# A three-block network on one core: bias broadcast, first recurrence factors, gla's log decay, mLSTM heads and a head norm moved

## The chip, the cores and the metric

One core of a Trainium2 chip runs the whole program as one launch. The time is the device time of that core in microseconds (us). The kernel before took 3819.36, 3821.92 and 3830.99 us in three runs, median 3821.92.

## The reference

Batch 1, 512 tokens, 1024 features, float32. Three blocks follow one another. The first puts 16 meta tokens ahead (528 in all) and merges an RWKV-7 recurrence with differential attention, then an MLP. The second has a gated convolution and a sparse attention with position biases. The third mixes an mLSTM, a gated linear attention (gla) and a gated delta net, then an MLP. What matters here, cut down:

```python
# block 1, RWKV-7: per head a 64x64 state over 528 tokens
S = S * w_t + (S a_t) b_t^T + v_t k_t^T;   y_t = S r_t
# block 2: position bias of a head at a distance
bias = rel_bias[t5_bucket(distance)]
# block 3, mLSTM (4 heads of 128): weights from scalar gates, divided by their sum
h = sigmoid(mo) * mlstm(q / sqrt(128), k, v, li, log_sigmoid(lf));  h = head_rmsnorm(h)
# block 3, gla: log decay per feature and token, summed along the tokens
lg = log_sigmoid(llr @ w_gla_lr + b_gla) / 16;   b = cumsum(lg)
S = exp(b_L) * S + sum_s (k_s * exp(b_L - b_s)) v_s^T
```

## The kernel before

Activations lie with features on the 128 partitions and tokens along them. A matmul of full precision is made of three of rounded float32 (h_hi by whi, h_lo by whi, h_hi by wlo): ACT rounds a slab of weights of 8 x 128 x 128 (whi), VectorE or POOL makes the rest (wlo). The program is a row of stages; each ends with a barrier of all engines, and inside one the engines wait on semaphores. Each engine takes its instructions in the order in which they are written; DMAs are issued from SP's queue, some from ACT's.

**opening** (L1898) loads x on SP, norms it and writes the pair h. Three small tables on ACT's queue give, by TensorE, the biases by distance (`row`, 8 heads x 640) and by residue (`cmp_row`). SP waits for `row` and writes it to DRAM 128 times over (`far`, 2.6 MB, from 8 partitions, L1928), then `near` (L1930). ACT squares x, copies the rows, makes the root, issues eleven loads of constants (L1964), and then makes the eight h_hi copies (L1967). VectorE's products (L1991) and low parts (L1988) alternate with these.

**rwkv_project** (L569) makes 27 projection tiles of 528 tokens: three for the low-rank inputs, then three (r, k, v) for each of eight groups of two heads. SP's queue carries for each group i: three weights for group i+2 (L612; one of them into the buffer `first`), a wait for the group's factors, the stores of factors, bonus and gate (L630 to L632), and the vectors of group i+2 (L615, L616). ACT rounds the weights (L723) between the evictions of tiles (L731) and the group's sigmoids, gate copy (L757), exponentials (L759 to L762) and root (L764). VectorE makes the factors and the bonus (L785 to L821); POOL the wlo.

**rwkv_tiles** (L825) runs the recurrence in chunks of 64 tokens. SP loads the factors of a group into one of three buffers f (L890, L891), after VectorE has padded them (L1181); TensorE transposes them first (L907).

**chain** (L97) is the helper for all later projections: slabs of weights in a ring of buffers, TensorE in slab order (L233), whi (L249) and wlo (L331) two or three slabs ahead, eviction of a tile with its scale by VectorE (L381). A `side` object puts further steps behind each slab s on TensorE, ACT and VectorE. HeadNorm (L1467) is one: it norms mLSTM's four heads in the last chain: square by ACT at s = 0, 3, 6, 9 (L1492), sum by TensorE at the same s (L1483), mean (L1503) and root (L1495) at s + 1, reciprocal and product (L1506, L1510) at s + 2. GateRows (L2296) is another, in the chain ahead of gla: it makes the scalar gates of four heads.

**gla** (L2480) starts with the log decay: TensorE's four products of 16 rows (L2541), bias (L2692), Abs, Exp and Ln by ACT (L2625 to L2629), scaling and four scans (L2697 to L2700), the far factors (L2703, L2634, L2706), then seven levels of decays. Of a level the argument is made by VectorE or POOL (L2527), two exponentials by ACT (L2640, L2641), two products by VectorE (L2711, L2712). ACT copies values (vt, L2632) and keys (kt, L2657), VectorE sums up the states (L2734 to L2736).

**mlstm** (L2362) runs four heads in a loop. POOL copies the head's keys, values, selector and scaled queries (L2423 to L2426); TensorE spreads the gate rows (L2395, L2396), transposes the values, makes four scores (L2404) and four pairs of values (ps_o L2412, ps_d L2413); ACT makes em, vt, four exponentials and one sigmoid; VectorE the arguments (L2456), weights (L2463) and the division (L2467 to L2471). POOL and TensorE begin the next head when `done` is reached:

```python
                with pe.Fori(0, 4) as h:
                    pe.wait_ge(fixed, h + 1)
                    pe.wait_ge(done, h)
```

## Time and profile before

| | |
|---|---|
| runs | 3819.36, 3821.92, 3830.99 us |
| profiled execution | 3828.68 us, span 3826.9 us |
| TensorE matmul busy | 3395.8 us (89%) |
| TensorE weight load busy | 2776.4 us (73%) |
| VectorE busy | 2032.3 us (53%) |
| ACT busy | 1235.7 us (32%) |
| POOL busy | 214.0 us (6%) |
| mean granted TensorE clock | 0.922 |

The profile is of one execution. Busy time is the sum of an engine's instructions; the busiest engine needn't be what a given stage waits for, so each stage is read for itself. A granted clock of 1.00 is 2.4 GHz, 0.50 is 1.2 GHz. The stages of interest lie at 0 to 75.9 us (opening), 75.9 to 309 (projections), 309 to 615 (recurrence), 2566 to 2681 (the chain ahead of gla), 2682 to 2787 (gla), 2970 to 3052 (mlstm) and from 3180 on (the last chain).

### The profile page before, as it was taken

To read this page: it belongs to the slowest core of one execution; us is meant where nothing else is said; L and a number is where in the kernel's file an instruction comes from. 1 tells how busy PE (TensorE), PEld (TensorE's weight loads), DVE (VectorE), ACT (ScalarE), POOL (GpSimd) and SP (SyncE) were. 2 spreads that over 40 slices of the span, in tenths; PEclk is the share of its full clock that TensorE was granted. 3 is DMA by queue.
4 is the path that set the end of the run, shared out by engine and by line. 5 is a ranking of instruction groups with operands and counts; after the bars stand their busy time and mean duration, and the time that the engine had idled before them with its cause. 6 is when DMAs were issued, how large, how long until landed. Compare 5 with 4: busy or idle time off the path is not lost. (4 is left out here: it accounts for less than half of the span.)

```text
span 3826.9 us, 57163 instructions
## 1 busy us (share of the span) xinstructions
PE 3395.8 (89%) x24046; PEld 2776.4 (73%) x24046; DVE 2032.3 (53%) x3290; ACT 1235.7 (32%) x2144; POOL 214.0 (6%) x187
## 2 busy tenths in 40 slices
PE   2996899988999999989999998969499698999998
PEld 1986888955888887757777777857378386878886
DVE  2885564555355344676546775354646445465342
ACT  2552233345333233223333222232422324333231
POOL 1321220010000000000000000000100120000000
PEclk9997898988999999975799999989699689999999
DMA  5332112201222322610122223322022002232221
GB/s 114 119 140 68 46 32 91 88 1 39 94 93 94 99 94 69 172 35 12 45 78 88 88 88 94 93 65 72 2 88 91 0 2 83 77 106 95 97 99 56
DMA packets 99340, 287.81 MB, mean 75 GB/s; under 512 B 19618, under 2 KB 23842, under 8 KB 97040
## 3 DMA queue, kind: packets, MB, share of 16 engines
q1 hardware_dynamic: 92456, 268.71, 21.9%
q10 hardware_dynamic: 6632, 15.47, 1.6%
q8 instruction: 191, 3.13, 0.3%
q14 instruction: 61, 0.50, 0.0%
HBM read 264.22 MB, written 19.89 MB: 74 GB/s over the span
## 5 line engine op out<-in xcount | busy, mean ns | idle before, releaser
L233 PE MATMUL acc<-h_hi,whi 128*128 128x512 f32 x1992 | 800.9, 402 | 74.4 <-DVE wlo L425 50.2
L233 PE MATMUL acc<-h_hi,wlo 128*128 128x512 f32 x1992 | 791.6, 397 | 0.0
L233 PE MATMUL acc<-h_lo,whi 128*128 128x512 f32 x1928 | 769.9, 399 | 0.0
L233 PEld LDWEIGHTS acc<-h_hi,whi 128*128 128x128 f32 x1992 | 379.1, 190 | 184.2 <-DVE wlo L425 52.6
L331 DVE TENSOR_TENSOR wlo<-wbuf,whi 128x1024 fp32r<-128x1024 f32 (+3 forms) x277 | 318.6, 1150 | 268.6 <-ACT whi L249 266.0
L233 PEld LDWEIGHTS acc<-h_hi,wlo 128*128 128x128 f32 x1992 | 379.4, 190 | 87.8
L233 PEld LDWEIGHTS acc<-h_lo,whi 128*128 128x128 f32 x1928 | 367.0, 190 | 86.9 <-issue 3.1
L249 ACT ACTIVATE whi<-wbuf 128x1024 fp32r<-128x1024 f32 (+3 forms) x277 | 274.5, 991 | 358.5 <-PE acc L233 335.3
L233 PE MATMUL acc<-arena_round,whi 128*128 128x512 f32 x736 | 236.9, 393 | 4.8 <-DVE arena_round L391 4.8
L331 DVE TENSOR_TENSOR wlo<-ahead,whi 128x1024 fp32r<-128x1024 f32 (+3 forms) x132 | 152.3, 1154 | 137.0 <-ACT whi L249 136.3
L249 ACT ACTIVATE whi<-ahead 128x1024 fp32r<-128x1024 f32 (+3 forms) x132 | 131.4, 996 | 178.6 <-PE acc L233 173.1
L658 PE MATMUL acc<-h_hi,whi 128*128 128x264 f32 x432 | 127.9, 296 | 65.2 <-POOL wlo L646 65.2
L233 PEld LDWEIGHTS acc<-arena_round,whi 128*128 128x128 f32 x736 | 139.4, 190 | 34.9 <-DVE arena_round L391 5.7
L233 PE MATMUL acc<-arena_round,wlo 128*128 128x512 f32 x416 | 162.9, 392 | 0.0
L233 PE MATMUL acc<-gates_round,whi 128*128 128x512 f32 x384 | 141.2, 395 | 3.0 <-DVE gates_round L391 1.8
L397 DVE TENSOR_TENSOR x<-acc,x 128x512 f32<-128x512 f32 x64 | 44.3, 692 | 178.4 <-PE acc L233 178.4
L658 PEld LDWEIGHTS acc<-h_hi,whi 128*128 128x128 f32 x432 | 83.0, 192 | 69.1 <-POOL wlo L646 65.9
L233 PE MATMUL acc<-gates_round,wlo 128*128 128x512 f32 x320 | 125.5, 392 | 0.0
L658 PE MATMUL acc<-h_lo,whi 128*128 128x264 f32 x432 | 123.9, 287 | 0.0
L658 PE MATMUL acc<-h_hi,wlo 128*128 128x264 f32 x432 | 123.9, 287 | 0.0
L1415 PE MATMUL acc<-h_hi,whi 128*128 128x264 f32 x384 | 115.9, 302 | 1.2 <-DVE wlo L1453 1.2
L282 ACT ACTIVATE val<-tmp 128x512 f32<-128x512 f32 x64 | 40.5, 632 | 216.7 <-DVE tmp L393 216.7
(730 smaller groups left out, 6365.6 us busy)
## 6 DMA issues: line engine op xcount, KB each, us to landing
wbuf<-in_mlp_out SPq DMA_DIRECT2D x46, 512.0 KB, 3.3
wbuf<-in_mlp_in SPq DMA_DIRECT2D x45, 512.0 KB, 3.3
wbuf<-in_w_gates SPq DMA_DIRECT2D x38, 512.0 KB, 3.4
wbuf<-in_ffn_up SPq DMA_DIRECT2D x29, 512.0 KB, 3.4
wbuf<-in_w_qkv SPq DMA_DIRECT2D x23, 512.0 KB, 3.6
rwkv_factors<-factors SPq DMA_DIRECT2D x8, 1320.0 KB, 4.6
f<-rwkv_factors SPq DMA_DIRECT2D x8, 1280.0 KB, 6.7
ahead<-in_mlp_in SPq DMA_DIRECT2D x19, 512.0 KB
```

The source lines that it names most:

```text
L233: mm = nc.tensor.matmul(acc[t % NB][:, 0:T], wt[s % ring][:, k - a, :], xt, start=(kx == 0 and q == 0), stop=(kx == job.K - 1 and q == 2))
L249: copy(whi[s % ring][:, 0:size(s), :], wbuf[s % ring][:, 0:size(s), :], ACT.Copy).then_inc(hi_ready, 1)
L282: copy(val[t % 2][:], tmp[t % 2][:], ACT.Square)
L331: TT(wlo[s % ring][:, 0:size(s), :], wbuf[s % ring][:, 0:size(s), :], whi[s % ring][:, 0:size(s), :].bitcast(F32), ALU.subtract).then_inc( ...
L397: TT(job.dst[n], ps, job.other[n], ALU.add).then_inc(evicted_d, 1)
L658: mm = nc.tensor.matmul(acc[n % 2][:, hf, 0:H], wt[n % R][:, kx, :], xt[:, kx, at], start=(kx == 0 and q == 0), stop=(kx == 7 and q == 2))
L1415: mm = nc.tensor.matmul(acc[n % NB][:, h, 0:H], wt[n % R][:, k, :], xt[:, k, h * H:(h + 1) * H], start=(k == 0 and q == 0), stop=(k == 7 a ...
```

## The change

- `far` isn't written in the opening. `row` stays resident, and rwkv_project writes it in eight pieces of 16 copies, each behind the stores of a group on SP's queue.
- The eleven constants are loaded by SP, behind `first`, instead of by ACT.
- The first group's factors are loaded at the end of rwkv_project into `early`, which lies in the place of y's tiles 2 to 7; POOL pads it. rwkv_tiles loads groups 1 to 7 only, and its memset of y goes.
- HeadNorm's sum moves to s + 1, mean and root to s + 2, reciprocal and product to s + 3.
- gla's log decay is made by a new side object, GlaGates, in the chain ahead of gla, in the places of z and o that are still free; GateRows' scratch moves into z too.
- mlstm's loop is written out with the heads overlapped; POOL's copies go, the scaling is in the weights, and the sigmoid is one instruction.

```diff
 # rwkv_project, SP
                     sp.dma_start(gate_scr[:, i, :], gates[i % 2][:]).then_inc(stored[i % 2], 16)
+                    sp.dma_start(far[:, 16 * i:16 * i + 16, :], row[:].rearrange("h (a w) -> h a w", a=1).broadcast_to([8, 16, 640])).then_inc(far_out, 16)
                     if i + 2 < 8:
                         vectors(i + 2)
+                sp.dma_start(early[:, :, 0:RM], fac_scr[0, :, :, 0:RM]).then_inc(early_in, 16)
+                sp.dma_start(early[:, :, RM + 48:], fac_scr[0, :, :, RM:T1]).then_inc(early_in, 16)
+                sp.wait_ge(early_in, 32)
                 for b in range(2):
                     sp.wait_ge(stored[b], 4 * 48)
+                sp.wait_ge(far_out, 16 * 8)
 # rwkv_tiles
+        def f_of(i):
+            return early if i == 0 else fs[i % 3]
-                for i in range(8):
-                    f = fs[i % 3]
-                    if i >= 3:
+                for i in range(1, 8):
+                    f = f_of(i)
+                    if i > 3:
                         sp.wait_ge(y_out, 2 * (i - 2))
-                nc.vector.memset(y[:, :, 0:RM], 0.0)
 # HeadNorm
-        if s < 12 and s % 3 == 0:
+        if s < 12 and s % 3 == 1:
             pe.wait_ge(self.sq_ready, s // 3 + 1)
...
-        elif s < 12 and s % 3 == 2:
+        elif 0 < s < 13 and s % 3 == 0:
+            h -= 1
             dve.wait_ge(self.root_ready, h + 1)
 # opening
-                sp.wait_ge(row_out, 1)
-                sp.dma_start(far, row[:].rearrange("h (a w) -> h a w", a=1).broadcast_to([8, P, W])).then_inc(stored, 16)
+                for name in names:
+                    sp.dma_start(c[name][:], a[name]).then_inc(const_in, 16)
...
-                for name in names:
-                    act.dma_start(c[name][:], a[name]).then_inc(const_in, 16)
 # GlaGates, a new side (ACT's DMAs of its weights at s = 2 left out)
+    def pe(self, pe, s, stat):
+        if s in (6, 8):
...
+            for q in range(2):
+                h = s - 6 + q
+                mm = self.nc.tensor.matmul(stat[q][:], self.wl[:, h * P:(h + 1) * P], self.lr, start=True, stop=True)
+    def act(self, act, s):
+        elif s == 9:
+            act.wait_ge(self.lin_ready, 4)
+            copy(pos, self.lin, ACT.Abs).then_inc(self.abs_ready, 1)
+            act.wait_ge(self.abs_ready, 1)
+            copy(pos, pos, ACT.Exp, scale=-1.0).then_inc(self.pow_ready, 1)
+        elif s == 10:
+            copy(pos, pos, ACT.Ln, bias=1.0).then_inc(self.ln_ready, 1)
+        elif s == 14:
+            copy(self.far[:], self.far[:], ACT.Exp).then_inc(self.far_exp, 1)
+            copy(self.dec[:], self.cum[:].rearrange("p h (n t) -> p h n t", t=GW)[:, :, :, GW - 1], ACT.Exp)
+    def dve(self, dve, s):        # s: what
+        # 7, 9: bias, two heads each   8: queries scaled   11: STT and the factor 1/16
+        # 12, 13: two scans each       14: far's argument  16: far times the keys
 # mlstm, TensorE
+                prelude(0)
+                scores(0, 0)
+                scores(0, 1)
+                for h in range(4):
+                    values(h, 0)
+                    scores(h, 2)
+                    values(h, 1)
+                    scores(h, 3)
+                    if h < 3:
+                        prelude(h + 1)
+                    values(h, 2)
+                    if h < 3:
+                        scores(h + 1, 0)
+                    values(h, 3)
+                    if h < 3:
+                        scores(h + 1, 1)
 # mlstm, ACT: sigmoid of all four heads first, then per head em, vt and four exponentials
+                copy(z[:, 12:16, :], z[:, 12:16, :], ACT.Sigmoid).then_inc(sig_ready, 1)
 # mlstm, VectorE
+                rows_of(0)
+                args(0, 0)
+                args(0, 1)
+                for h in range(4):
+                    weights(h, 0)
+                    args(h, 2)
+                    weights(h, 1)
+                    args(h, 3)
+                    weights(h, 2)
+                    if h < 3:
+                        rows_of(h + 1)
+                        args(h + 1, 0)
+                    weights(h, 3)
+                    if h < 3:
+                        args(h + 1, 1)
+                    divide(h)
```

`prelude` is the two spreads of gate rows and the transposes of the values; em, vt and mb have two buffers now, ps_o and ps_d one, and `values(h, 0)` waits for `done` of the head before. In gla all that the new side makes is gone, with its waits: TensorE begins with the transposes of the values, ACT with their copies, VectorE with the argument of level 0.

## Rows read from the trace of the kernel before

**Rows 1.** Timeline of the opening: start, duration (us), engine, line, operation, [idle before]

```profile
11.50 0.85 SPq L1928 DMA_DIRECT2D bias_by_distance<-row  x1
...
12.97 19.01 SPq L1930 DMA_DIRECT2D bias_by_residue<-cmp_row  x1
...
19.26 1.45 DVE L1991 SCALAR_TENSOR_TENSOR squares<-x,norm_w,rstd 128x528 f32<-128x528 f32 x2
...
64.98 1.18 ACT L1967 ACTIVATE h_hi<-squares 128x528 fp32r<-128x528 f32 x2 [49.24 <-issue]
...
75.93 0.36 SPq L612 DMA_DIRECT2D wbuf<-in_w_rwkv  x1
```

**Rows 2.** DMA queues from 20 to 60 us: queue, packets, MB, share

```profile
q1 hardware_dynamic: 768, 1.97, 46.6%
```

**Rows 3.** Projections, one group's timeline, and ACT's idle time before L723

```profile
187.33 0.33 SPq L630 DMA_DIRECT2D rwkv_factors<-factors  x1
...
197.71 1.06 ACT L723 ACTIVATE whi<-first 128x1024 fp32r<-128x1024 f32 x1 [2.46 <-DMA first<-in_w_rwkv]
...
211.06 0.71 DVE L821 TENSOR_TENSOR bonus<-za,factors 128x528 f32<-128x528 f32 x1
...
  DMA first<-in_w_rwkv: 6.9, 5
```

**Rows 4.** Timeline from the projections to the recurrence

```profile
301.78 0.32 SPq L630 DMA_DIRECT2D rwkv_factors<-factors  x1
...
308.95 0.77 DVE L1181 MEMSET f<- 128x240 f32 x3 [7.20 <-PEq L42]
...
309.75 0.62 SPq L890 DMA_DIRECT2D f<-rwkv_factors  x1
...
317.28 1.97 PE L907 MATMUL psA<-ident,f 128*128 128x128 f32 x8 [22.07 <-DMA f<-rwkv_factors]
```

**Rows 5.** Busy time by stretch: length, PE, PEld, DVE, ACT, POOL, PEclk, DMA share, GB/s

```profile
2640.00:2660.00 20.00, 20.00 (x88) 16.17 (x87) 7.56 (x8) 4.25 (x4) 0.00 (x0) 1.00 0.26 87
2681.00:2720.00 39.00, 11.58 (x25) 5.75 (x26) 22.54 (x15) 14.50 (x13) 7.59 (x2) 0.53 0.01 1
```

**Rows 6.** Timeline: end of the chain ahead of gla, and gla's start

```profile
2680.08 0.69 DVE L381 TENSOR_TENSOR z<-acc,scale 128x512 f32<-128x512 f32 x1 [4.88 <-PE acc L233]
...
2681.69 1.80 POOL L2678 MEMSET scores<- 128x2048 f32 x1 [1801.46 <-POOLq L42]
...
2684.22 5.48 PE L2541 MATMUL psL<-small,wl 16*128 16x512 f32 x6 [4.18 <-DMA w<-in_norm_gla]
...
2701.18 1.07 ACT L2632 ACTIVATE vt<-psT 128x512 f32<-128x512 f32 x2
...
2711.71 5.77 DVE L2527 TENSOR_TENSOR ring<-cum 128x2048 f32<-128x2048 f32 x1
...
2719.60 1.21 DVE L2711 TENSOR_TENSOR ring<-ring,z 128x1024 f32<-128x1024 f32 x1
...
2728.12 2.29 DVE L2527 TENSOR_TENSOR ring<-cum 128x2048 f32<-128x2048 f32 x1
```

**Rows 7.** mlstm: timeline of a head, and the clock of one stretch

```profile
2972.67 1.47 PE L2395 MATMUL ps_b<-rows,sel 4*128 4x512 f32 x2 [2.48 <-POOL qs L2426]
...
2985.16 0.69 DVE L2467 TENSOR_TENSOR den<-ps_d,em 128x512 f32<-128x512 f32 x1 [1.11 <-PE ps_d L2413]
...
2991.68 2.04 PE L2395 MATMUL ps_b<-rows,sel 4*128 4x512 f32 x2 [6.65 <-DVE o_m_plain L2471]
...
3005.20 0.69 DVE L2467 TENSOR_TENSOR den<-ps_d,em 128x512 f32<-128x512 f32 x1 [1.11 <-PE ps_d L2413]
...
3000.00:3002.00 2.00, 2.00 (x6) 1.03 (x5) 0.35 (x2) 1.47 (x3) 0.00 (x0) 0.84 0.00 0
```

**Rows 8.** Last chain: waits (total, times, longest), and a stretch

```profile
PE stat L1483 <- ACT sums L1492: 10.1, 4, 3.0
...
3192.00:3195.00 3.00, 3.00 (x7) 1.87 (x6) 1.23 (x1) 0.35 (x1) 0.00 (x0) 0.50 0.37 122
```

More of the change, by code:

```diff
@@ L566, with rwkv_project @@
 LEVELS1 = math.ceil(math.log2(RC))
-def rwkv_project(nc, c, w, first, h, fac_scr, chunk_decay, bonus_scr, gate_scr):
+def rwkv_project(nc, c, w, first, row, far, h, fac_scr, early, chunk_decay, bonus_scr, gate_scr):
     NT, R = 27, 3
@@ L1895, in dve, with opening @@
                 TT(self.a[:, i, :], self.a[:, i, :], self.rstd[:], ALU.mult).then_inc(self.norm_ready, 1)
-def opening(nc, a, c, both, x, h, far, near, first):
+def opening(nc, a, c, both, x, h, row, near, first):
     H = T1 // 2
-    W = far.shape[2]
+    W = row.shape[1]
     M = near.shape[1] * near.shape[2]
@@ L1957, in _ @@
                 act.wait_ge(rows_ready, 1)
-                copy(row[:].rearrange("h (a w) -> h a w", a=2), ps_r[0:8, :, 0:W // 2], ACT.Copy).then_inc(row_out, 1)
+                copy(row[:].rearrange("h (a w) -> h a w", a=2), ps_r[0:8, :, 0:W // 2], ACT.Copy)
                 act.wait_ge(rows_ready, 2)
@@ L2330, in act @@
             act.wait_ge(self.end_ready, 1)
-            copy(rows[:, 7, :], self.end[:], ACT.Exp)
+            copy(rows[:, 7, :], self.end, ACT.Exp).then_inc(self.exp_done, 1)
     def dve(self, dve, s):
@@ L2386, in _, with prelude, scores, values @@
             def _(pe):
+                def prelude(h):
+                    if h > 0:
+                        pe.wait_ge(mb_ready, h)
+                    nc.tensor.matmul(ps_b[:], c["head_sel"][:, h, :], rows[:, 1, :], start=True, stop=True).then_inc(b_ready, 1)
+                    if h > 0:
+                        pe.wait_ge(em_ready, h)
+                    nc.tensor.matmul(ps_e[:], c["head_sel"][:, h, :], rows[:, 2, :], start=True, stop=True).then_inc(e_ready, 1)
+                    if h > 0:
+                        pe.wait_ge(v_copied, h)
+                    for j in range(TN):
+                        mm = nc.tensor.transpose(ps_v[:, j * P:(j + 1) * P], z[:, 8 + h, j * P:(j + 1) * P], c["ident"][:])
+                    mm.then_inc(v_ready, 1)
+                def scores(h, j):
+                    g = TN * h + j
+                    if g > 1:
+                        pe.wait_ge(pt_ready, g - 1)
+                    nc.tensor.matmul(ps_k[g % 2][:, 0:T2 - j * P], z[:, 4 + h, j * P:(j + 1) * P], z[:, h, j * P:T2], start=True,
+                                     stop=True).then_inc(kq_ready, 1)
+                def values(h, j):
+                    g, n = TN * h + j, T2 - j * P
+                    if j == 0:
+                        pe.wait_ge(v_copied, h + 1)
+                        if h > 0:
+                            pe.wait_ge(done, h)
+                    pe.wait_ge(pt_ready, g + 1)
+                    nc.tensor.matmul(ps_o[:, j * P:T2], vt[h % 2][:, j * P:(j + 1) * P], pt[g % 2][:, 0:n], start=(j == 0), stop=(j == TN - 1))
+                    nc.tensor.matmul(ps_d[:, j * P:T2], c["ones"][:], pt[g % 2][:, 0:n], start=(j == 0), stop=(j == TN - 1)).then_inc(o_ready, 1)
                 for j in range(TN):
@@ new lines, in _, with prelude @@
+                copy(z[:, 12:16, :], z[:, 12:16, :], ACT.Sigmoid).then_inc(sig_ready, 1)
+                def prelude(h):
+                    act.wait_ge(e_ready, h + 1)
+                    if h > 1:
+                        act.wait_ge(done, h - 1)
+                    copy(em[h % 2][:], ps_e[:], ACT.Exp).then_inc(em_ready, 1)
+                    act.wait_ge(v_ready, h + 1)
+                    if h > 1:
+                        act.wait_ge(o_ready, TN * (h - 1))
+                    copy(vt[h % 2][:], ps_v[:], ACT.Copy).then_inc(v_copied, 1)
@@ L2471, in _ @@
                     TT(o[:, h, :], ps_o[:], den[:], ALU.mult).then_inc(done, 1)
-                    chain.close()
+                    dve.wait_ge(done, h + 1)
+                rows_of(0)
+                args(0, 0)
+                args(0, 1)
+                for h in range(4):
+                    weights(h, 0)
[7 more added lines that the diff above has]
+                    weights(h, 3)
+                    if h < 3:
+                        args(h + 1, 1)
+                    divide(h)
@@ L3242, in first_block @@
             decay = resident(nc, m2, "chunk_decay", [P, 8, RN + 1])
+            early = y[:, 2:8, :].rearrange("p k t -> p (k t)")[:, 0:5 * (RM + 48 + RN * RC)].rearrange("p (f t) -> p f t", f=5)
             with ExitStack() as m3:
                 first = resident(nc, m3, "first", [P, 8, P])
-                opening(nc, a, c, both, x, h, far, near, first)
-                rwkv_project(nc, c, a["w_rwkv_1"], first, h, factors, decay, bonus, gate)
-            rwkv_tiles(nc, c, y, factors, decay)
+                row = resident(nc, m3, "row", [8, 640])
+                opening(nc, a, c, both, x, h, row, near, first)
+                rwkv_project(nc, c, a["w_rwkv_1"], first, row, far, h, factors, early, decay, bonus, gate)
+            rwkv_tiles(nc, c, y, factors, early, decay)
         o, o_lo = overlaid(nc, m, "o", [P, 8, T2])
```

298 lines of the change are left out of this document (145 added, 153 removed).

## The prediction

> **What bounds the kernel now.** I read the page's engine table first. TensorE is busy 3395.8 us of 3826.9 (the table above), so an edit pays only where TensorE waits, or where a stage has little for it. Then I read timeline and waits of each stage that the diff touches, asking which wait ends last.
>
> In the opening, `row` (the biases by distance) leaves by one DMA at 11.50, and the next issue on SP's queue takes 19.01 us. ACT has eleven loads of constants to issue ahead of its h_hi copies; these start at 64.98, though VectorE had the input of the first ready half way through its row at 19.26. The projections begin at 75.93 [rows 1]. No engine bounds this stage; the broadcast does: from 20 to 60 us its queue moved 768 packets [rows 2], 19.2 per us.
>
> In the projections a tile takes about 24 us, and the loop is tight: SP issues the stores of a tile (187.33), then vectors, then weights; ACT waits for the weights in `first` until 197.71, and only behind that copy come the exponentials that VectorE needs; VectorE's bonus ends at 211.77. ACT waited for this DMA five times, in all five tiles that have it [rows 3]. So its landing already sets the time of such a tile.
>
> **The change part by part.** The profiled execution took 3828.68 us (its span 3826.9), 6.8 above the median of 3821.92; I take differences from its rows and apply them to the median.
>
> *Opening.* ACT issues no constants, and no broadcast is in flight. VectorE's first product is there at 20.0, so h_hi starts at some 20.1 instead of 64.98, and what hangs on it, up to 75.93, follows at the same distance: **-44.9**. Eleven loads move to SP behind `first`: at up to 0.85 us an issue [rows 1] they are out within 10 us of x's, and their 1.6 MB lands before VectorE's last low part near 30, which covers them. Without that cover they would cost perhaps 5.
>
> *Broadcast in eight pieces.* A piece has 8 x 16 packets of the same 2,560 bytes, from the same eight partitions: 128 packets at 19.2 per us are 6.67 us. It stands on SP's queue behind a tile's stores and ahead of its vectors and weights. Bounds of the delay to `first`: 0, if it trickles beside them, and 19.0, if an issue behind it blocks as in [rows 1]. I take 6.67, since what is queued must drain either way, and 128 packets do that in it. ACT is in order: behind its wait for `first` stand the gate copy, both exponentials and the root for kn; VectorE waits for those, SP's next stores for VectorE. In the tile of [rows 3] `first` comes 10.4 after the stores, and from there to the bonus's end it is 14.1; a later landing moves those 14.1 whole. Five tiles (behind the last three pieces no weights follow): 5 x 6.67 = **+33.4**. TensorE idles longer in them; a fallen clock would add up to 2 a tile, which goes into the range.
>
> By the Trainium skill (DMA: Bandwidth & Descriptors, Queues, rings and completion order) each DMA engine takes the descriptors of one issuer's ring in order, which speaks against this place for the pieces; by it the delay is the whole piece, and if the trace of after shows the weights landing as early as now, the sum lacks the 33.4. The Trainium skill (SBUF — State Buffer, Door 1) gives about 27 GB/s for each port that a DMA's partitions reach, and two ports for partitions 0 to 7: an estimate of 6.0 us a piece and 30 in all, where the row says 33.4.
>
> *Early factors.* Before, the last stores are issued at 301.78, the next stage's VectorE starts at 308.95, its first load is issued at 309.75 and its first transpose runs at 317.28, after that DMA [rows 4]: 15.5 us. Now a piece (6.7) and the early load stand behind the stores (about 6.0 to land, as the stage then ends). Of the 7.5 from that load's issue to the transpose I take 5, since it queues behind others, and 1.8 for the change of stage: 19.5, **+4**. Bounds: -3, if the piece runs beside the stores, and +7. The memset of y that goes and the padding that POOL gains lie under other waits and cost nothing, less than 0.3 uncovered. The later factors had no wait in the trace and get none.
>
> *Log decay.* Slabs of this chain are 5.57 us apart (0.69 of eviction and 4.88 idle before it [rows 6]), TensorE full; VectorE is busy 7.56 and ACT 4.25 of 20 us. What moves is most of gla's first 39 us: 22.54 of VectorE less the 5.77 of a level's argument that stays, 16.8, and some 10 of ACT's 14.50 [rows 5, 6]. Over nine slabs (50 us) that fits between low parts, which are made two slabs ahead: 0, and about 2 without that slack. TensorE's four products do come onto its path: three took 5.48 at half clock [rows 6], so four take 7.3 there and **+3.7** at full. In gla the first products of level 0 came at 2719.60, 37.9 after a start at 2681.7 [rows 6]. Now VectorE begins with the level's argument (2.29 where POOL isn't beside it, as at 2728.12). ACT makes four vt copies behind the transposes (some 4.5 us from the start: two took 1.07, and they alternate with as long transposes) and two exponentials (2.1, from the argument's end at 2717.48 to the products): products at +6.6, that is 31.3 earlier. The states after them no longer wait for kt's source; they end 1.2 earlier still. Net 3.7 - 32.5 = **-28.8**, between -24 and -31.
>
> *mLSTM heads.* A head takes 20.04 us (2985.16 to 3005.20): 6.5 of division with TensorE idle, then 13.5 of TensorE with hardly a gap, at half clock (1.2 GHz) until inside 3000 to 3002 and full (2.4 GHz) after [rows 7]. The next head's values still wait for `done`, as ps_o and ps_d are single. So on the path stay the division, all values, scores 2 and 3, and the next head's prelude and score 0, which are only issued earlier, ahead of the last values. Score 1 goes under the division (384 columns where 512 took 2.04 at half clock, so about 0.8 at full); the first weights (an operation of 512 like the 0.69 of [rows 7], and a hop), which lay beside TensorE's work, step onto the path. Nothing per head. At the start POOL's copies go (TensorE waited 2.48), but ACT now makes the whole sigmoid with two table loads ahead of em: of the 2.5 about 1.4 is left, **-1**. Bounds: -16, if the clock stays full, and +5, if ACT's new order holds up the first head.
>
> *Head norm.* TensorE waits for ACT's squares four times, 10.1 us in all, and runs at 0.50 for 3 us after the first [rows 8], which costs 1.5. A slab later the squares are ready; root and reciprocal keep their distance. **-11.5**.
>
> Sum: -44.9 + 33.4 + 4 - 28.8 - 1 - 11.5 = -48.8, so **3773** from the median.
>
> **Rivals.**
> *The pieces hide.* They run beside the weights. For: the old broadcast let ACT's loads through while it ran. Against: same queue, ahead of the weights, and ACT's waits of [rows 3]. Price: the 33.4 fall out, and some 4 at the hand-over: 3736.
> *mLSTM at full clock.* For: the next prelude lengthens each burst of TensorE. Against: the pause stays 6.5. Half of the some 9 us at half clock, four times, with a bit lost to VectorE: 16 in all, 3757.
> *Slower than before.* Each piece blocks SP's queue like the issue of 19.01 us, with vectors and weights behind it, in the five tiles. With a delay d they cost 5d, against 82.2 gained elsewhere: it decides from d = 16.4, and is slower by over 0.3% from 18.7. At 20 us: +17.8, 3840. Against: an eighth of the packets drains in a third of that.
> *The opening stays long*, because another load holds ACT. Nothing else is issued there on ACT's queue between x and h_hi; I give it nothing.
>
> **How the numbers follow.** Forecast 0.73, pieces hidden 0.14, full clock 0.10, slower 0.03. The likeliest gives 3773. Its bounds: a delay of 5 to 9 a tile (-8, +12), half clock in the projections (+10), gla and mLSTM (-10, +8). The range reaches down to the first rival and up to 3797. About 0.3% (11.5 us) is what a measurement of this kernel can tell from no change. The first three cases are faster, with 0.02 of them left for an unforeseen gap that ends within 0.3%: 0.95, 0.02, 0.03.
>
> **What would show it.** The projections start near 31. Their tiles 1 to 5 take 30 us instead of 24, with ACT waiting some 8 us for `first` in each, and the last two stay. The first transpose of the recurrence comes 19 to 20 after the last stores. gla's first products come 6 to 7 after its start, and its chain has four products more and no new gap. A head of mLSTM stays near 20, at half clock after each division. The last chain has no wait on squares. I am wrong if the tiles stay at 24, if a gap opens in the gla chain near slabs 9 to 12, or if the heads fall to 16.

## The result, and the profile of the changed kernel

The changed kernel takes 3765.22 us (median of four runs, 3757.46 to 3779.03), the kernel before 3822.6 on the same chip: a ratio of 0.9849, 95% interval 0.982 to 0.9879, so 57.4 us less. The forecast was 48.8 less (3773). The profiled execution took 3757.46 us (span 3755.7), the fastest of its four, where the profiled one of before took 3828.68: the two traces differ by 71.2, more than the medians.

To see where it went, I took in both traces the time at which each stage starts and subtracted. Stage lengths are in us; "forecast" is the term of the sum.

| stretch | before | after | difference | forecast |
|---|---|---|---|---|
| start to the projections | 75.9 | 31.4 | -44.5 | -44.9 |
| projections: five groups with weights behind the piece | 119.6 | 156.6 | +37.0 | +33.4 |
| projections: last two groups | 41.6 | 43.3 | +1.7 | 0 |
| last stores to first transpose | 15.5 | 17.9 | +2.4 | +4 |
| product ahead of gla, and gla | 221.4 | 189.1 | -32.2 | -28.8 |
| product ahead of mLSTM, and mLSTM | 265.6 | 256.4 | -9.1 | -1 |
| last product (head norm) | 624.0 | 611.0 | -13.1 | -11.5 |
| all other stages together | | | -13.4 | 0 |

The touched stretches sum to -57.8, close to the 57.4 of the medians. The last row I don't count to the change. Its largest entries are a stage at 1689 us (183.1 before, 177.6 after), the recurrence behind its first transpose (297.3, 293.8) and the stage behind mLSTM (127.2, 124.2). In the kernels tried below, which leave the code of these stretches as it is in the changed kernel, they took 177.6 to 186.0, 294.0 to 297.3 and 121.6 to 128.7.

The touched stretches scatter too, so each difference is that of one pair of traces. The five groups took 151.2 to 156.6 in the eight traces that have the pieces in this place and size. mLSTM itself is 83.2 before and 73.1 after. Of eight other kernels with the same mLSTM four took 73.0 and four 76.0; in these four the clock granted to TensorE falls 3.6 us after the stage's first product and is at half for 10.2 us, where in the others it falls 0.6 to 0.7 after it and is at half for 6.8.

**Opening** (answers to [rows 1]). Timeline of the changed kernel: start, duration, engine, line, operation, [idle before].

```profile
20.47 1.32 ACT L1978 ACTIVATE h_hi<-squares 128x528 fp32r<-128x528 f32 x2 [4.33 <-DVE squares L2001]
...
31.39 0.83 SPq L614 DMA_DIRECT2D wbuf<-in_w_rwkv  x2
```

ACT's first high part comes at 20.47 instead of 64.98, and waits only for VectorE. In the kernel before, beside the broadcast, ACT's loads of constants (twelve by the trace, where I had counted eleven) were slow to issue, 3.9 to 4.8 us each from the second on:

```profile
15.50 4.72 ACTq L1964 DMA_DIRECT2D ident<-in_ident  x1
...
61.07 3.86 ACTq L1964 DMA_DIRECT2D rope_swap<-in_rope_swap  x1
```

**Projections** (to [rows 3]). Timeline of SP's queue and of ACT in one group, then ACT's waits from 90 to 320 us (total, times, longest).

```profile
126.52 0.33 SPq L632 DMA_DIRECT2D rwkv_factors<-factors  x1
...
128.32 1.31 SPq L635 DMA_DIRECT2D bias_by_distance<-row  x1
129.68 1.26 SPq L617 DMA_DIRECT2D vec<-in_rwkv_vec  x1
130.98 3.38 SPq L618 DMA_DIRECT2D lora_w<-in_lora_up  x1
134.41 3.04 SPq L614 DMA_DIRECT2D first<-in_w_rwkv  x1
...
143.56 1.06 ACT L731 ACTIVATE whi<-first 128x1024 fp32r<-128x1024 f32 x1 [7.61 <-DMA first<-in_w_rwkv]
...
ACT whi L731 <- DMA first<-in_w_rwkv: 29.1, 5, 7.6
```

The weights in `first` serve ACT 17.0 us after the group's stores (10.4 before), and it waited 29.1 us for them where it waited 6.9. On average of the five groups they come 15.2 us after the stores (9.6 before). SP's issues behind the piece also take longer, 3.38 and 3.04 us.

That is 5.6 us a group; the other 1.8 lie between ACT's copy of `first` and the next stores, which takes 16.2 us on average (14.3 before). ACT's operations up to `kn` and VectorE's behind them wait for TensorE nowhere in that stretch. In each of the five groups one of VectorE's operations behind `kn` takes 2.7 to 2.9 us where it takes 0.7 alone, while POOL makes a low part beside it:

```profile
151.59 4.65 POOL L654 TENSOR_TENSOR wlo<-wbuf,whi 128x1024 fp32r<-128x1024 f32 x2 [4.53 <-ACT whi L731]
...
154.06 2.76 DVE L823 TENSOR_TENSOR kn<-kn,kk 128x528 f32<-128x528 f32 x1
```

In the group of [rows 3] the same product (L815) took 0.71 us; it took 1.02 and 1.66 in two others, beside such a low part. ACT rounds the second and third weight of the group 2.2 us apart now (150.45 and 152.67), since what it has to evict ahead of them became ready while it waited; in a group before they came 6.7 apart (180.37 and 187.09). So the low part falls among VectorE's last operations ahead of the stores. In one group of the eight traces it didn't (m2_prelude_in_pause, from 141.5 us), and the stretch took 14.1 us; in all others it took 16.1 to 16.2.

**Hand-over** (to [rows 4]). Same view.

```profile
295.84 0.32 SPq L632 DMA_DIRECT2D rwkv_factors<-factors  x1
...
298.96 1.28 SPq L638 DMA_DIRECT2D y_plain<-rwkv_factors  x1
300.28 4.22 SPq L639 DMA_DIRECT2D y_plain<-rwkv_factors  x1
...
313.77 1.94 PE L919 MATMUL psA<-ident,y_plain 128*128 128x128 f32 x8 [24.52 <-PEq L42]
```

**Start of gla** (to [rows 6]). VectorE goes straight to the first level's argument, and has its products 5.1 us after the stage's first instruction, where it was 37.9.

```profile
2670.13 1.80 POOL L2803 MEMSET scores<- 128x2048 f32 x1 [1796.78 <-POOLq L42]
2670.17 2.29 DVE L2674 TENSOR_TENSOR ring<-cum 128x2048 f32<-128x2048 f32 x1 [1.03 <-PEq L42]
...
2675.19 1.90 DVE L2819 TENSOR_TENSOR ring<-ring,z 128x1024 f32<-128x1024 f32 x1 [2.73 <-ACT ring L2766]
```

**mLSTM** (to [rows 7]). Timeline of two divisions, then the stretch around the second (columns as in [rows 5]).

```profile
2946.30 0.69 DVE L2604 TENSOR_TENSOR den<-den,z_m 128x512 f32<-128x512 f32 x1
...
2948.59 2.05 PE L2516 MATMUL ps_o<-pt,vt 128*128 128x512 f32 x2 [6.51 <-DVE pt L2593]
...
2964.09 0.69 DVE L2604 TENSOR_TENSOR den<-den,z_m 128x512 f32<-128x512 f32 x1
...
2962.00:2966.00 4.00, 0.00 (x0) 0.00 (x0) 3.90 (x4) 0.00 (x0) 0.00 (x0) 0.62 0.00 0
2966.00:2970.00 4.00, 3.62 (x5) 1.64 (x6) 1.42 (x4) 0.91 (x2) 0.00 (x0) 0.52 0.02 4
2970.00:2974.00 4.00, 4.00 (x15) 2.05 (x14) 1.33 (x3) 0.08 (x1) 0.00 (x0) 1.00 0.00 0
```

TensorE still pauses 6.5 us, but the clock is full again some 4 us after it resumes (2966.4 to 2969.8), where it had been some 9. After the three divisions it ran at half clock for 4.2, 3.4 and 3.1 us; before, for 8.9, 9.4 and 9.6. The divisions lie 17.8, 17.4 and 13.9 us apart (20.0, 20.3 and 20.4 before). In the last chain TensorE's waits list no `sums` any more ([rows 8]), only those of 4.8 and 4.1 us that both kernels have.

### The profile page after: what moved, and what is told of

The parts are those of the page before. It is cut to its first block and busy times, and to the rows that moved or that the text cites. A ratio compares the mean times of both kernels' runs of the same rounds, so it can differ in the third digit from the quotient of the medians.

```text
span 3755.7 us, 56986 instructions
## 1 busy us (share of the span) xinstructions
PE 3377.5 (90%) x24046; PEld 2765.4 (74%) x24046; DVE 2021.5 (54%) x3289; ACT 1225.3 (33%) x2135; POOL 201.8 (5%) x171
## 5 line engine op out<-in xcount | busy, mean ns | idle before, releaser
L233 PEld LDWEIGHTS acc<-h_hi,whi 128*128 128x128 f32 x1992 | 378.9, 190 | 183.4 <-DVE wlo L425 52.9
L666 PE MATMUL acc<-h_lo,whi 128*128 128x264 f32 x432 | 125.4, 290 | 0.0
L1426 PE MATMUL acc<-h_lo,whi 128*128 128x264 f32 x384 | 109.6, 286 | 0.0
```

Source lines behind the costliest of these rows:

```text
L233: mm = nc.tensor.matmul(acc[t % NB][:, 0:T], wt[s % ring][:, k - a, :], xt, start=(kx == 0 and q == 0), stop=(kx == job.K - 1 and q == 2))
L666: mm = nc.tensor.matmul(acc[n % 2][:, hf, 0:H], wt[n % R][:, kx, :], xt[:, kx, at], start=(kx == 0 and q == 0), stop=(kx == 7 and q == 2))
L1426: mm = nc.tensor.matmul(acc[n % NB][:, h, 0:H], wt[n % R][:, k, :], xt[:, k, h * H:(h + 1) * H], start=(k == 0 and q == 0), stop=(k == 7 a ...
```

## The experiments

Each kernel is the changed kernel with the edit named. Two questions led: what in the pieces costs 37 us, and why mLSTM gained nine times what I gave it.

### Where a piece stands in the queue

```diff
@@ p1_pieces_behind
                 for n in group(i + 2): weight(n)
+                sp.dma_start(far[:, 16 * i:16 * i + 16, :], ...)
                 sp.wait_ge(fac_ready, i + 1)
...
-                sp.dma_start(far[:, 16 * i:16 * i + 16, :], ...)
@@ p2_weights_ahead
-                for n in group(i + 2): weight(n)
+                for n in [*(group(2) if i == 0 else ()), *group(i + 3)]: weight(n)
                 sp.wait_ge(fac_ready, i + 1)
```

> Each piece of the broadcast is issued behind the three weights of its tile, ahead of the wait for the tile's factors, instead of behind the stores; nothing else differs from the changed kernel, in which five groups take 156.6 us (31.3 each, 23.9 before) and ACT waits 7.6 us at the longest for the weights in the first buffer. Theory A (order): the cost is that the weights stand behind the piece's packets in the queue. Then ACT's wait falls back to some 2.5 us, the five groups to about 120 to 124, and the time by 33 to 37 us, to about 3730. Theory B (shared bandwidth): the piece slows whatever moves beside it, wherever it stands. Then the stores, issued some 17 us later, meet no piece, but the second and third weight do; ACT waits for those instead, and at most 15 us come back, to about 3750 or above. Slower than the changed kernel by neither.

Measured: 3721.6 us, ratio 0.9733 (0.9704 to 0.9763). ACT's waits:

```profile
ACT whi L731 <- DMA first<-in_w_rwkv: 7.7, 5, 2.2
```

The five groups take 118.4 us, the wait is back where it was (7.7 in all, 6.9 before), and the piece, in flight beside nothing urgent, costs nothing. It was the order. The medians differ by 43.6 rather than 37. By the traces the five groups are 38.2 shorter, the last two groups 1.6, and from the last stores to the first transpose it is 11.1 us instead of 17.9, because the last piece now stands ahead of those stores.

> The three weights of a tile are issued one tile earlier, as soon as their buffers are free, ahead of the wait for the factors and the stores; the pieces stay where they are, behind the stores and ahead of the vectors. Theory A (order): the piece now delays only the stores' followers that nobody waits for, so the whole 37 us come back, and with them the waits of 2.5 us for the weights that the kernel before already had, five times: about 45 to 49 us less than the changed kernel's 3765, some 3718, with tiles of 21 to 22 us. Theory B (shared bandwidth): the weights, moved out of the piece's time, are not slowed either; the same. Rival C: the vectors and the product of the next tile (they stand behind the piece) are the next to be late; they were issued two tiles ahead, so I give that little: then a wait for the vectors appears in front of the first product of a tile, and the time stays above 3740.

Measured: 3720.9 us, ratio 0.9728 (0.9697 to 0.9759). ACT doesn't wait for a weight's DMA at all, but its copies of `first` are 23.2 us apart, not 21 to 22. The vectors aren't late either (C). The reason stands in the busy time of the projections, columns as in [rows 5]; first the changed kernel, then this one:

```profile
95.00:255.00 160.00, 121.89 (x850) 113.40 (x850) 105.54 (x126) 69.01 (x89) 38.78 (x16) 0.90 0.42 130
```

```profile
95.00:255.00 160.00, 140.25 (x1032) 131.78 (x1032) 150.57 (x169) 87.07 (x111) 40.99 (x16) 0.97 0.50 152
```

VectorE was busy 105.5 of 160 us while ACT waited; without the wait it is busy 150.6, 94%, and from 95 to 195 us, the stretch of the groups with weights, its list of waits is empty: it is the bound. So of the waits that were left, only some 0.5 us a tile is won over the run with the piece behind the weights (23.7 us a tile).

### How long a piece is, and what makes it so

```diff
@@ p3_half_pieces
-                    sp.dma_start(far[:, 16 * i:16 * i + 16, :], row ... broadcast_to([8, 16, 640]))
+                    at, rows_ = (8 * i, 8) if i < 5 else (40 + 30 * (i - 5), 30 if i < 7 else 28)
+                    sp.dma_start(far[:, at:at + rows_, :], row ... broadcast_to([8, rows_, 640]))
@@ p4_pieces_from_dram
+                sp.dma_start(row_d, row[:]).then_inc(row_out, 16)
...
-                    sp.dma_start(far[:, 16 * i:16 * i + 16, :], row[:].rearrange(...)...)
+                    sp.dma_start(far[:, 16 * i:16 * i + 16, :], row_d.rearrange(...)...)
```

> The same place in the queue, but pieces of 8 rows instead of 16 in the first five tiles, and of 30, 30 and 28 in the last three, behind which no weights follow. It measures the slope. Theory A (queue drained in order at 19.2 packets per us): 64 packets are 3.3 us instead of 6.7, so the five groups take 18 us less than 156.6, about 138 to 140; the last three pieces drain beside a tile each (12.5 us), the last of them ahead of the early factors, where it adds 5 at the hand-over: 13 less in all, about 3752. Theory D (a fixed price for each issue of such a broadcast, as the 19 us of one issue in the opening of the kernel before): the groups stay at 150 or above, and the time at 3760 or above.

Measured: 3751.9 us, ratio 0.9807 (0.9778 to 0.9836). The five groups take 134.5, less than theory A had (138 to 140), the hand-over 21.9.

```profile
ACT whi L732 <- DMA first<-in_w_rwkv: 16.2, 5, 4.8
```

With 0, 8 and 16 rows ahead of the weights the five groups take 118.4, 134.5 and 156.6, that is 3.2 and 7.6 a tile. No fixed price of an issue (D): it is the packets. The trace's packet records say the same: the 64 packets of such a piece take 3.3 us from the first to the last, and the 128 of a piece of the changed kernel 6.5 to 6.6, in every tile.

> The row of biases is written to DRAM once at the start of the projections (20 KB), and the pieces read it there, with the same 8 x 16 packets of 2,560 bytes at the same place in the queue. Theory E (the source limits a piece: eight SBUF partitions deliver some 49 GB/s): with a source in DRAM a piece drains in 2 us or less, ACT's wait for the weights falls from 7.6 to about 3 to 4, the five groups from 156.6 to 123 to 130, and the time to about 3735. The Trainium skill (SBUF — State Buffer, Door 1) says the same of partitions 0 to 7, which by it share two ports. Theory F (the eight DMA engines limit it: the queue's busy share was 46.6% while the broadcast ran in the kernel before, as if half of the 16 worked): the piece is as long as before, the groups stay at 150 or above, 3760 or above. The Trainium skill (DMA: Bandwidth & Descriptors, Quick rules) bears on F: an outermost dimension of fewer than 16 keeps a DMA to so many engines.

(The section meant is that page's Rules for kernel authors.) Measured: 3726.1 us, ratio 0.9747 (0.9714 to 0.9779); the five groups 123.4 us, the hand-over 13.1.

```profile
ACT whi L735 <- DMA first<-in_w_rwkv: 9.8, 5, 2.5
```

Theory E. By the packet records the same 128 packets take 1.8 to 2.2 us from DRAM; a packet occupies its engine 102 ns (median), where one from SBUF takes 392 at the same place in the queue. Both kinds keep some seven engines busy at once, so a restriction to eight engines holds in both and isn't the bound (F falls). While a piece leaves SBUF the queue moves little, as the stretch from 167 to 171 us of the changed kernel shows (queue, packets, MB, share of 16 engines):

```profile
q1 hardware_dynamic: 147, 0.29, 54.0%
```

That is 73 GB/s with the other DMAs' first packets in it; 320 KB in 6.55 us are 50. The Trainium skill (SBUF — State Buffer, Door 1) gives 27 GB/s for each of the two ports that partitions 0 to 7 reach, 54 in all: the trace agrees to within a tenth. Not all records look like that, though. Where the pieces stand behind three weights (p1_pieces_behind), those of five groups span only 4.0 to 4.4 us, with medians of 102 to 108 ns a packet, though the source is the same. Such a piece is issued well ahead of its first packet (at 101.35, the packets run from 105.43 to 109.83), so it may have been read from SBUF in part while the weights were still landing; no run tests that. So the 392 ns are shown for a piece that drains with little ahead of it, and the ports as their cause are not shown by themselves.

### The opening and the early factors

```diff
@@ o1_constants_on_act: the loop over the loads, SP's queue
-                for name in names: sp.dma_start(c[name][:], a[name])
@@ and ACT's, between the root and the high parts
+                for name in names: act.dma_start(c[name][:], a[name])
@@ n1_no_early_load: end of the projections, and the recurrence's loop
-                sp.dma_start(early[:, :, 0:RM], fac_scr[0, :, :, 0:RM]).then_inc(early_in, 16)
-                sp.dma_start(early[:, :, RM + 48:], fac_scr[0, :, :, RM:T1]).then_inc(early_in, 16)
-                sp.wait_ge(early_in, 32)
...
-                for i in range(1, 8):
+                for i in range(8):
```

> In the opening the eleven loads of constants go back to ACT's queue, between its root and its copies of the high part, where the kernel before had them; the broadcast is still in pieces in the projections. It tells which of the two moves gave the 44.5 us. Theory A (the issues were slow because the broadcast filled the rings, as the one of 19.01 us on SP): alone, eleven issues at 0.43 to 0.85 are 5 to 9 us ahead of the first high part, and the projections start at 36 to 41 instead of 31.4: 3771 to 3775. Theory B (issuing on ACT is slow by itself): the start goes back above 60, 3795 or more.

Measured: 3761.5 us, ratio 0.9848 (0.9828 to 0.9869); the projections start at 32.6. Rows of ACT's queue:

```profile
15.97 0.36 ACTq L1975 DMA_DIRECT2D norms<-in_norms  x1
...
21.19 0.45 ACTq L1975 DMA_DIRECT2D rope_swap<-in_rope_swap  x1
21.69 1.18 ACT L1978 ACTIVATE h_hi<-squares 128x528 fp32r<-128x528 f32 x2 [5.08 <-DVE squares L2001]
```

Theory A, and less than it allowed (36 to 41): the twelve take 5.7 us, most of it under VectorE's reciprocal. The projections start 1.2 us later than in the changed kernel, 0.5 of which was there before the first issue (the root begins at 15.97, at 15.50 in the changed kernel); the kernels with the loads on SP start at 30.7 to 32.2. So of the 44.5 us the missing broadcast gives at least 43.3, and moving the loads at most 1.2.

> The first factors are loaded by the recurrence itself, as in the kernel before (with the clearing of its output), not ahead of its start; the pieces stay. From the last stores to the first transpose it is 15.5 us before, 17.9 in the changed kernel, and 11.1 where no piece stands ahead of the early load. Theory A (the early load gains what it moves ahead of the change of stage, and the piece takes more): the piece has drained by the time that the recurrence issues its load, 8 us after the last stores, so the hand-over is 15.5 to 17.5, and the early load is worth nothing or slightly less than nothing here: 3763 to 3767. Theory B (the early load is worth its 4 us in spite of the piece): 20 to 22, and 3768 or above. The median can't tell it; the trace does.

Measured: 3768.4 us, ratio 0.9857 (0.9837 to 0.9878).

```profile
293.91 0.32 SPq L632 DMA_DIRECT2D rwkv_factors<-factors  x1
...
307.43 0.77 DVE L1185 MEMSET f<- 128x240 f32 x3 [13.54 <-PEq L42]
308.23 0.62 SPq L894 DMA_DIRECT2D f<-rwkv_factors  x1
...
315.60 1.97 PE L911 MATMUL psA<-ident,f 128*128 128x128 f32 x8 [28.26 <-DMA f<-rwkv_factors]
```

Theory B: 21.7 us. I had overlooked that the stage ends only when the last piece has landed: VectorE starts the next one 13.5 us after the last stores, 7.2 in [rows 4], and the load is issued after that. So the last piece costs 6.2 to 6.8 (21.7 against 15.5; 17.9 against 11.1), and the early load gains 3.8 with a piece and 4.4 without.

### mLSTM: order or clock

```diff
@@ m1_filled_pause (FILL = 5) and m3_pause_filled_to_end (FILL = 8)
                         scores(h + 1, 1)
+                        for _ in range(FILL):
+                            nc.tensor.matmul(ps_x[:], c["ones"][:], z[:, 0, :], start=True, stop=True)
@@ m2_prelude_in_pause
                     if h < 3:
-                        prelude(h + 1)
+                        maxima(h + 1)
                     values(h, 2)
-                    if h < 3: scores(h + 1, 0)
                     values(h, 3)
                     if h < 3:
+                        prelude(h + 1); scores(h + 1, 0)
                         scores(h + 1, 1)
```

> In the mLSTM of the changed kernel five products of 512 columns that nobody reads follow the last one ahead of each division (three times), into a bank of their own; nothing else differs. The divisions of the changed kernel lie 17.8, 17.4 and 13.9 us apart where the kernel before had 20.04, and the granted clock is 0.50 from 3 us into the pause of 6.5 until some 4 us after it. Theory A (the clock alone sets the difference to 20.04): TensorE's work of a head is the same, and with the pause filled the clock stays at 2.4 GHz, so the 4.1 us at half clock become 2: the divisions lie 15.7, 15.4 and 13 to 14 apart, 4 to 6 us less in all, 3759 to 3761. Theory B (the order of the work sets it, the clock is incidental): the distances stay at 17.4 or more. Either is near the 0.3% that a median can tell, so the trace decides: the windows of the clock and the distances of the divisions.

Measured: 3767.2 us, ratio 0.9858 (0.9839 to 0.9877); divisions 17.4, 17.4 and 14.0 apart, as theory B had it. But the clock fell all the same:

```profile
2948.82 4.45 PE L2541 MATMUL ps_x<-z_m,ones 128*128 128x512 f32 x10
...
2955.49 1.46 PE L2517 MATMUL ps_o<-pt,vt 128*128 128x512 f32 x2 [2.23 <-DVE pt L2596]
...
2952.00:2956.00 4.00, 1.77 (x5) 0.50 (x4) 3.86 (x6) 0.16 (x1) 0.00 (x0) 1.00 0.00 0
2956.00:2960.00 4.00, 4.00 (x8) 2.07 (x7) 0.96 (x3) 0.75 (x2) 0.00 (x0) 0.57 0.00 0
```

It was at 1.2 GHz for most of the four microseconds after a pause of 2.2, so the run doesn't test A; it only says that this filler was too short.

> As the run with five products in each pause of the mLSTM, but with eight. Five lasted 4.45 us and left 2.2 of pause; the clock fell all the same, 3 us after they ended, and the divisions stayed 17.4 apart. Eight last 7.1 us and leave no pause, but hold back the next values by up to 0.6. Theory A (any pause of some 2 us lets the clock fall, and the time at half clock is what a head loses): the granted clock stays 1.00 between the divisions and they lie 16.0 to 16.6 apart. Theory G (the clock falls there whatever TensorE does, products that nobody reads included): 0.50 shows in the windows as before, and they lie 17.5 to 18.2 apart. The sum is 3 to 4 us less or 1 to 2 more than with five, which a median can't tell.

Measured: 3764.2 us, ratio 0.9849 (0.9834 to 0.9864).

```profile
2940.80 7.03 PE L2541 MATMUL ps_x<-z_m,ones 128*128 128x512 f32 x16
...
2945.20 0.69 DVE L2607 TENSOR_TENSOR den<-den,z_m 128x512 f32<-128x512 f32 x1
...
2944.00:2948.00 4.00, 4.00 (x10) 1.71 (x9) 3.86 (x6) 0.17 (x1) 0.00 (x0) 1.00 0.00 0
2948.00:2952.00 4.00, 4.00 (x14) 2.23 (x13) 0.98 (x3) 0.74 (x2) 0.00 (x0) 1.00 0.00 0
2952.00:2956.00 4.00, 4.00 (x19) 2.42 (x18) 2.14 (x4) 2.29 (x4) 0.00 (x0) 1.00 0.00 0
```

The clock stays full, and the divisions lie 15.8, 15.8 and 12.5 apart. From the end of the last slab's eviction to the last product of the last division it is 67.4 us, 72.3 in the changed kernel, 82.6 before. The whole kernel's median doesn't show these 5 us. With products that nobody reads, and nothing else changed, the heads shorten by nearly the time that TensorE had lost at half clock: by 1.9, 1.6 and 1.4 us, where half of the 4.2, 3.4 and 3.1 us is 2.1, 1.7 and 1.5. G falls.

> Of the next head's prelude only the maxima stay ahead of the last two values; the stabilisers, the transposes of v and the first scores (1.0 + 0.66 + 1.0 us at full clock) are issued behind the last values, ahead of the second scores, so they run while VectorE divides. Theory A: TensorE's path of a head loses these 2.7 us, and its pause shrinks from 6.5 to some 3.5, so that the clock falls later or not at all: the divisions lie 13 to 15 us apart, and the time falls by 8 to 13, to 3752 to 3757. Rival: the weights of the next head's first scores, which need its exponentials and these scores, are late behind the division on VectorE: then TensorE waits longer than until the division's end, and less than 5 come back, 3760 or above.

Measured: 3764.6 us, ratio 0.9855 (0.9836 to 0.9874), no gain that the median shows. The divisions are 17.1, 17.1 and 14.9 apart; from the last slab it is 71.2 us, 1.1 less. The pause did shrink to 4.0, but TensorE then ran at half clock for 5 us instead of 4, and the last weights of a head came late:

```profile
2959.44 0.69 DVE L2588 TENSOR_TENSOR ex<-mask_st,mb 128x512 f32<-128x512 f32 x1
2960.05 0.28 DVE L2596 SCALAR_TENSOR_TENSOR pt<-ps_k,ex 128x128 f32<-128x128 f32 x1
...
2960.39 0.49 PE L2518 MATMUL ps_o<-pt,vt 128*128 128x128 f32 x2 [0.65 <-DVE pt L2596]
```

VectorE makes the next head's maxima and argument ahead of them, which TensorE's prelude had covered. So the 2.7 us moved under the division came back as a wait and as time at half clock.

### Parts taken back, and the best order

```diff
@@ m4_heads_back: the function mlstm is that of the kernel before
@@ g1_decay_back: GlaGates is not used, the function gla is that of the kernel before
@@ b1_order_and_handover
+                for n in [*(group(2) if i == 0 else ()), *group(i + 3)]: weight(n)
...
                     if i + 2 < 8: vectors(i + 2)
+                    if i < 7:
+                        at, rows_ = (19 * i, 19) if i < 2 else (38 + 18 * (i - 2), 18)
+                        sp.dma_start(far[:, at:at + rows_, :], ...)
```

> The mLSTM is that of the kernel before (heads one after the other, sigmoid, values and scaled queries prepared for each head), in the changed kernel. If the part is worth what the two traces show (9.6 us from the last slab's eviction to the last division: 81.9 before, 72.3 after), the divisions lie 20.0 apart again, with TensorE some 9 us at half clock in each head, and the time is 3773 to 3776. If the shorter heads came from where the clock stood when the stage began, and not from the part, they lie 17 to 18 apart here too, and the time stays at 3765.

Measured: 3780.6 us, ratio 0.9888 (0.9873 to 0.9903). The divisions are 20.1, 20.3 and 20.4 apart, 82.7 us from the last slab (the 81.9 of the expectation, by the same reading, is 82.6), and TensorE is at half clock for most of 9 us after each division again, as in this stretch after it resumed at 2954.86:

```profile
2958.00:2962.00 4.00, 4.00 (x9) 1.92 (x8) 2.45 (x4) 2.42 (x4) 0.00 (x0) 0.50 0.00 0
2962.00:2966.00 4.00, 4.00 (x10) 2.12 (x10) 1.79 (x5) 2.79 (x4) 0.00 (x0) 0.76 0.00 0
```

So the shorter heads belong to the part. Its median is 15 us above the changed kernel's, though, more than the 10 of the stage. Against the changed kernel's trace the product and mLSTM are 9.2 longer; the rest of that trace's excess stands in stages with the same code (8.4 in the one at 1689 us, 4.5 in the one after mLSTM). The latter has hardly to do with mLSTM: that stage took 121.6 to 127.3 in kernels with the new mLSTM, and 127.2 in the kernel before.

> The log decay of the gated linear attention is computed at the start of its stage again, as in the kernel before, and not beside the product ahead of it; the rest is the changed kernel. Predicted for the part: 28.8; the two traces differ by 32.2 over the product and the stage (2.2 more in the product, 34.5 less in the stage). If the part alone does that, the time is 3794 to 3798, and from the stage's start to its first products it is 38 us again instead of 5.

Measured: 3796.8 us, ratio 0.9936 (0.992 to 0.9951): 31.6 above the changed kernel, as the traces had it. First products come at

```profile
2705.08 1.21 DVE L2862 TENSOR_TENSOR ring<-ring,z 128x1024 f32<-128x1024 f32 x1
```

37.9 us after the stage's first compute instruction at 2667.16. The product ahead of it is back at 115.7 us, as before; with the log decay in it, it took 116.8 to 118.5.

> Weights ahead of the stores, and the pieces behind the vectors, the broadcast being spread over the first seven tiles (19, 19 and five of 18 rows), so that none stands ahead of the early factors; the rest is the changed kernel. By the runs so far: the order gives 44 (3721), and the hand-over falls from 17.9 to the 11.1 that stood where no piece was ahead of the early load, so 7 more: 3714, between 3709 and 3719. If VectorE, busy 150 of 160 us in the projections once the waits are gone, is the bound there, the tiles stay 23.2 apart; a rival is that the longer pieces (7.5 us) reach the next weights' issue and some of the wait comes back: then the tiles are 24 or more apart and the time is 3720 or more.

Measured: 3720.1 us (3712.07 to 3727.32, five runs), ratio 0.973 (0.9713 to 0.9747). The groups are 23.2 apart and the hand-over 11.2, as expected, and the first transpose runs at 264.5, 49.2 us earlier than in the changed kernel. The whole is 45 below it, not 51, outside the range that I gave, and can't be told from the two that differ only in the order (3721.6, 3720.9). Against the first of them I had counted the hand-over twice: with the piece behind the weights it was 11.1 already, and the first transpose ran at 265.8. Against the second the transpose is 6.2 us earlier (270.7), which the medians don't show. All three beat both kernels by more than the intervals; the simplest is the piece behind the weights.

## Why the prediction was right, and where its steps were off

*Opening*, -44.9 forecast, -44.5 measured. The step had two reasons, no constants on ACT and no broadcast in flight; the second is nearly all of it (43.3 or more): the broadcast in flight had made ACT's issues slow.

*Pieces*, +33.4 forecast, +37.0 measured. Place and order were right, and so was the length of a piece: 6.67 us from the rate of [rows 2], 6.5 to 6.6 in the packet records. The sum comes near for two reasons that offset each other. `first` came 5.6 us later on average, not 6.67: 27.8 in five groups. And what hangs behind it was not "moved whole": it became 1.8 us longer a group, 9.2 in all, by VectorE's operation beside POOL's low part, which the step had at nothing. TensorE's clock, which the range had, isn't needed for it, as nothing on the way from `first` to the stores waits for TensorE. "The pieces hide" (0.14) was wrong because of the place alone; behind the weights they do. "Each piece blocks SP's queue" from 16.4 us was far off: the longest issue behind a piece took 4.2 in the changed kernel.

*Early factors*, +4 forecast, +2.4 measured; the early load is worth -3.8 to -4.4, the last piece +6.2 to +6.8. The forecast had both, though its reason for the second was that the load queues behind it; n1 showed that the end of the stage waits for the piece as well.

*Log decay*, -28.8 forecast, -32.2 by the traces and -31.6 by the run that takes it back. The product became 2.2 longer, not 3.7 (its four new products are there, but TensorE waited 3.8 us for low parts where it had waited 5.7), the stage 34.5 shorter, not 32.5; the first products came at 5.1, not 6.6, after its start. No gap opened in the chain: it fits.

*mLSTM*, -1 forecast, -9.1 measured. This is the step that failed: "Nothing per head", with the second half of TensorE's work at full clock and the first at half as before. TensorE's work on the path was as I listed it. But at half clock it now runs 4.2, 3.4 and 3.1 us after the divisions instead of 8.9, 9.4 and 9.6; half of the difference is 8.7 us, of 10.3 that the stage lost by its last division (82.6 to 72.3). The last interval, 13.9 us, has no prelude in it, but that is no gain: the second head's prelude now stands ahead of the first division, which comes 1.4 us later after the last slab (17.7, 16.3 before) in spite of POOL's copies that went. I had the clock as a rival at 0.10, with 16 us for one that never falls. Its size was right: with the pause filled, mLSTM is 15.2 shorter than before (82.6 to 67.4). The change by itself got two thirds of it. The prediction named "the heads fall to 16" as a sign of error; they fell to 17.6. What lets the clock recover sooner in the new order isn't settled: no run changed only what TensorE does in the time ahead of the pause.

*Head norm*, -11.5 forecast, -13.1 by the traces; no run took it back alone, so of this part only the wait's disappearance is shown.

The errors of single terms (+0.4, +3.6, +1.7, -1.6, -3.4, -8.1, -1.6) cancel in part, by luck: 57.8 in place of 48.8. The upper bound, 3797, isn't what its own parts add up to (12, 10 and 8 above 3773 are 3803); the result lies far from either.

## What to carry to other kernels

Before a transfer is put into a queue, ask what is issued behind it and who waits for that. Here moving one issue behind the five that follow it was worth 44 us, as much as the opening had gained. Price a transfer by its own rows (packets and rate), but take what follows a longer wait from rows as well: here it came to lie beside POOL's work and became 1.8 us longer a group. When a wait goes, look which engine is then near 100%: that is where the gain will stop. Where TensorE pauses for a few microseconds, the pause is not the whole price; count the microseconds at half clock behind it too.

## What I had not expected of the hardware

At the same place in the queue a packet of 2,560 bytes took 392 ns when its source was one of eight SBUF partitions and 102 ns from DRAM; the 320 KB piece went from 6.55 to some 2 us. Behind the weights the records of SBUF packets were shorter too (4.0 to 4.4 us a piece), for a reason that is open. The kernel can use the DRAM source even without reordering: that run came within 6 us of the best order.

After a pause of 2.2 us that followed 4.45 us of filler, TensorE's clock fell to 1.2 GHz just the same; filled to the end for 7.03 us, it never fell between divisions.

Issues on SP's queue that stood behind a piece of 16 copies took up to 4.4 us, and 19.01 once behind the whole broadcast of [rows 1]. ACT's issues, on a queue of their own, took 3.9 to 4.8 us each beside that broadcast and 0.45 with none in flight.

One of VectorE's operations of 128x528 took 2.7 to 2.9 us where an operation of POOL's ran beside it, and 0.7 alone.
